# Expert results scattered by choice and token, the last two blocks added by products

## Chip, cores and metric

One core of a Trainium2 chip runs the whole program. The metric is the device time of one execution in microseconds (us).

## What is computed

Two model blocks on 512 tokens of 1024 columns, all in float32. The change touches only the last stage, a mixture of experts: each token picks a group out of 4, and in it the best 2 of 8 experts.

```python
w2 = jax.nn.softmax(top_v, axis=-1) * p_sel            # two shares a token
combine = jnp.sum(one_hot(expert_id, 32) * w2[..., None], axis=1)
for n in range(32):
    a, b = jnp.split(h @ w_up[n], 2, axis=-1)          # 1024 x 512
    out = out + combine[:, n:n + 1] * ((jax.nn.silu(a) * b) @ w_down[n])   # 256 x 1024
x = x + out
```

## The kernel before, in words

Tokens are sorted into *blocks* of up to 96 rows (`ROWS`) that share an expert: 32 first blocks, one for each expert, and up to ten more where an expert has over 96 tokens. With these inputs 32 blocks run: the loads of expert weights stand 32 times in the trace. Token numbers of the slots of all blocks come out of small products of one-hot matrices (`tokens`, L4227): those of the first blocks ahead of block 0, those of the blocks beyond behind block 3.

`experts` (L3999) is one block of five queues. Blocks 0 to 3 are written out (`STATIC`), then a loop on each engine runs pairs of blocks up to a register's value, then the last two, `step((before, 2, 4))` and `step((before, 3, 4))`, are written out again (`each_block`). A block n goes through these steps, spread over neighbouring steps of the loop:

- GpSimd gathers its 96 rows of the normalised tokens from DRAM by an indirect DMA (L4107); in the loop it copies the index column first (L4117). The gather of block n waits until the rows of block n-2 are turned.
- TensorE turns them (`turn_rows`, L4158), multiplies two of eight column groups as float32 (L4169), the other six as three products of a high and a low part (`product`, L399 to L401) with the up weights. ScalarE makes the high parts (L4268, L4276), VectorE the low ones (`rest`, L394).
- ScalarE takes silu, VectorE gates (L4375), TensorE turns the hidden rows (L4183), and `second` multiplies them with the split down weights into banks YB, YB+1.
- ScalarE copies the result to one of two buffers (`result`, L4307); SyncE stores the 96 rows contiguously to `expert_results` in DRAM (L4077), two steps later in its own queue, between the two loads of up weights for block n+2. `result` of n+2 waits for the store of n.

The up weights lie in a ring of two slots of 2 MB, the down weights in two more buffers. Behind the loop `rows_and_shares` (L3968, VectorE) works out in which row of `expert_results` each choice's result lies, and the two shares. Then the block of queues ends, and `combine` (L4428) opens another: GpSimd gathers for each of four token tiles and each of two choices 128 rows by `moe_row` into the ring (eight indirect loads, L4437), VectorE adds each times its share to x (L4448), SyncE stores each tile of x (L4457). The rows of `expert_results` for the ten possible blocks beyond are filled with finite numbers much earlier, by one DMA of 3840 KB in `project_out` (L655).

Of the kernel before, what the change touches and what calls it, by code (L numbers as in the profile page):

```python
# [599 lines left out]
def project_out(k, lhs, tiles, w, gain, next_gain, after=(), scratch=None, x_back=None, router=None):  # L600
# [38 lines left out]
    with ExitStack() as own:  # L639
# [6 lines left out]
        def _(sp):  # L646
# [3186 lines left out]
def number(k, r, pool):  # L3833
# [11 lines left out]
    count(r.sixteens[:, :], [[RUNS, RUN - 1]], RUNS)  # L3845
# [63 lines left out]
def layout(k, r, dve):  # L3909
# [18 lines left out]
    nc.vector.tensor_scalar(r.before_last[:, :], r.more_pairs[:, :], float(NE // 2 - 2), None, ALU.add)  # L3928
# [27 lines left out]
def slots_beyond(k, r, dve):  # L3956
# [8 lines left out]
    nc.vector.tensor_tensor(r.token_of_block[:, :, :], r.is_block[:, :, :], along(r.token_id, shape), ALU.mult).then_inc(r.slotted.sem, 1)  # L3965


def rows_and_shares(k, r, dve):  # L3968
# [4 lines left out]
    shape = [P, 2 * NT, RUN - 1]  # L3973
    nc.vector.tensor_tensor(r.over_one[:, :, :], along(r.rank, shape), across(r.sixteens, shape), ALU.is_gt)
    nc.vector.tensor_scalar(r.row_f[:, :], r.rank[:, :], -1.0, float(RUN), ALU.add, ALU.mult)
    dve.drain()
    nc.vector.tensor_reduce(r.full[:, :].rearrange("p (n o) -> p n o", o=1), r.over_one[:, :, :], AX.X, ALU.add)
    nc.vector.scalar_tensor_tensor(out=r.row_f[:, :], in0=r.block[:, :], scalar=float(ROWS), in1=r.row_f[:, :], op0=ALU.mult, op1=ALU.add)
    dve.drain()
    nc.vector.scalar_tensor_tensor(out=r.row_f[:, :], in0=r.full[:, :], scalar=1.0 - ROWS, in1=r.row_f[:, :], op0=ALU.mult, op1=ALU.add)  # L3980
# [8 lines left out]
    nc.vector.tensor_tensor(r.share2[:, :, :], r.share2[:, :, :], r.share1[:, :, :], ALU.mult)  # L3989

# [8 lines left out]
def experts(k, r, rows_dram, rows_stored, y_dram, up, dn, e):  # L3999
# [7 lines left out]
    XB, UB, YB, HB = 0, 2, 4, 6  # L4007

# [14 lines left out]
    def pair_before_last(queue):  # L4023
        return queue.value_load(r.before_last[0:1, 0:1], min_val=0, max_val=NB // 2 - 2)
# [15 lines left out]
    def later(n, d):  # L4040

        return (n[0], n[1] + d, n[2]) if isinstance(n, tuple) else n + d
# [553 lines left out]
```

## Time and profile before

| | |
|---|---|
| median of 3 runs | 2645.57 us (2643.05 to 2646.64) |
| profiled execution | 2643.07 us |
| its span in the profile | 2641.1 us |
| TensorE busy over the span | 94% |
| VectorE, ScalarE, GpSimd busy | 60%, 43%, 9% |
| expert stage and combine | about 2278 to 2641 us |

The span is what the profiler saw between the first and the last event; the execution's time lies 1.97 us over it. "PE" is TensorE's matrix products, "PEld" its weight loads, DVE is VectorE, ACT ScalarE, POOL GpSimd, SP SyncE. A line of a timeline gives start and duration in us, then engine, line of the kernel, operation and tensors.

### The profile page before, as it was taken

Reading aid. Unit: us, or ns where it says so; the run is one execution under the profiler, and the core shown is the slowest. Engines: PE = TensorE matmul, PEld = TensorE weight load, DVE = VectorE, ACT = ScalarE, POOL = GpSimd, SP = SyncE. Lnnn points to the kernel's source line nnn. Section 1 sums busy time; section 2 is a strip of 40 time slices with the busy share of each in tenths; the row PEclk is TensorE's granted clock in tenths of the full one; section 3 lists DMA queues with packets and bytes.
Section 4 is the critical chain, followed back from the end, with each engine's and each line's share of the span. In section 5 each row is a group of like instructions: output and inputs, shape, how many; then the busy total and the mean of one; then the engine's idle time right before and its main releaser. Section 6 shows DMA issues by size and latency. Waiting matters only on the chain. (4 is left out here: it accounts for less than half of the span.)

```text
span 2641.1 us, 32353 instructions
## 1 busy us (share of the span) xinstructions
PE 2495.4 (94%) x11409; PEld 1903.3 (72%) x11409; DVE 1587.7 (60%) x2386; ACT 1145.1 (43%) x1898; POOL 235.7 (9%) x237
## 2 busy tenths in 40 slices
PE   8999997799999999999999999999899899999995
PEld 6877785577888886766788888678757677666663
DVE  6766445745555525644655553548899656588784
ACT  5423332434444324623444442433333532377773
POOL 0000001000000000000000000345424000111111
PEclk9999999999999999999999999999999999999997
DMA  4321231032333321202233331322202004599995
GB/s 150 108 84 64 96 112 56 31 138 80 96 95 95 128 104 53 86 33 82 93 96 96 97 141 49 111 98 85 95 32 96 1 33 133 184 371 377 387 390 200
DMA packets 196720, 320.65 MB, mean 121 GB/s; under 512 B 16513, under 2 KB 112673, under 8 KB 196609
## 3 DMA queue, kind: packets, MB, share of 16 engines
q1 hardware_dynamic: 191678, 310.71, 34.1%
q0 software_dynamic: 4736, 8.40, 1.0%
q8 instruction: 69, 1.13, 0.2%
q14 instruction: 42, 0.34, 0.0%
q10 hardware_dynamic: 195, 0.06, 0.0%
HBM read 298.43 MB, written 29.10 MB: 124 GB/s over the span
## 5 line engine op out<-in xcount | busy, mean ns | idle before, releaser
L399 PE MATMUL ps<-ffn_parts 128*128 128x512 f32 x1056 | 411.6, 390 | 2.4 <-DVE ffn_parts L394 1.7
L401 PE MATMUL ps<-ffn_parts 128*128 128x512 f32 x1056 | 410.9, 389 | 0.0
L400 PE MATMUL ps<-ffn_parts 128*128 128x512 f32 x1056 | 410.8, 389 | 0.0
L399 PEld LDWEIGHTS ps<-ffn_parts 128*128 128x128 f32 x1056 | 198.2, 188 | 46.5 <-issue 2.6
L394 DVE TENSOR_TENSOR ffn_parts<-ring,ffn_parts 128x1024 fp32r<-128x1024 f32 x132 | 157.7, 1222 | 117.9 <-ACT ffn_parts L2454 107.4
L401 PEld LDWEIGHTS ps<-ffn_parts 128*128 128x128 f32 x1056 | 198.2, 188 | 41.3
L400 PEld LDWEIGHTS ps<-ffn_parts 128*128 128x128 f32 x1056 | 198.2, 188 | 40.9
L394 POOL TENSOR_TENSOR w_lo<-ring,w_hi 128x512 fp32r<-128x512 f32 (+1 forms) x112 | 161.0, 1442 | 720.8 <-ACT w_hi L558 720.4
L2505 DVE SCALAR_TENSOR_TENSOR y_tmp<-ps,pcol,y_tmp 128x511 f32<-128x511 f32 x88 | 61.9, 745 | 214.0 <-ACT y_tmp L2438 214.0
L1012 ACT CAST front_w_hi<-ring 128x512 fp32r<-128x512 f32 x104 | 64.1, 620 | 214.1 <-PE ps L401 214.0
L394 DVE TENSOR_TENSOR front_w_lo<-ring,front_w_hi 128x512 fp32r<-128x512 f32 x104 | 71.5, 688 | 131.5 <-ACT front_w_hi L1012 131.3
L558 ACT CAST w_hi<-ring 128x512 fp32r<-128x512 f32 (+1 forms) x112 | 68.2, 610 | 185.9 <-PE ps L401 178.4
L316 PE MATMUL ps<-brow,ident 128*128 128x512 f32 x248 | 121.4, 630 | 18.9 <-PEq L1938 4.8
L394 DVE TENSOR_TENSOR expert_up_lo<-ring,expert_up_hi 128x1024 fp32r<-128x1024 f32 x96 | 116.8, 1224 | 4.4 <-ACT expert_up_hi L4268 4.2
L3451 DVE SCALAR_TENSOR_TENSOR conv_gate<-conv_u,pcol,conv_gate 128x512 f32<-128x512 f32 x120 | 114.1, 998 | 2.2 <-issue 0.5
L2438 ACT ACTIVATE y_tmp<-ps,pcol 128x512 f32<-128x512 f32 x88 | 63.7, 774 | 109.7 <-PE ps L401 109.5
L4268 ACT CAST expert_up_hi<-ring 128x1024 fp32r<-128x1024 f32 x96 | 101.0, 1054 | 19.7 <-PE ps L401 17.4
L399 PE MATMUL ps<-kept_hi,w_hi 128*128 128x512 f32 x256 | 101.6, 397 | 3.7 <-POOL w_lo L394 2.5
L399 PE MATMUL ps<-front_h_hi,front_w_hi 128*128 128x512 f32 (+1 forms) x232 | 97.4, 420 | 3.8 <-ACT hst L1341 2.7
L399 PE MATMUL ps<-wo_hi,lhs_hi 128*128 128x512 f32 x256 | 100.7, 393 | 0.4 <-DVE lhs_lo L394 0.4
L400 PE MATMUL ps<-kept_lo,w_hi 128*128 128x512 f32 x256 | 100.5, 393 | 0.0
L401 PE MATMUL ps<-kept_hi,w_lo 128*128 128x512 f32 x256 | 100.4, 392 | 0.0
(666 smaller groups left out, 5561.9 us busy)
## 6 DMA issues: line engine op xcount, KB each, us to landing
ring<-in_w_up SPq DMA_DIRECT2D x32, 1536.0 KB, 9.4
ring<-in_ffn_w_up SPq DMA_DIRECT2D x88, 512.0 KB, 5.0
moe_down<-in_w_down SPq DMA_DIRECT2D x32, 1024.0 KB, 10.5
ring<-in_ab_w_in SPq DMA_DIRECT2D x13, 2048.0 KB, 7.9
ring<-in_w_in SPq DMA_DIRECT2D x11, 2048.0 KB, 7.8
ring<-in_ffn_w_down SPq DMA_DIRECT2D x10, 2048.0 KB, 7.7
ring<-in_w_up SPq DMA_DIRECT2D x32, 512.0 KB, 10.2
ring<-in_c_w_in SPq DMA_DIRECT2D x6, 2048.0 KB, 8.1
```

What stands on the lines that cost most here:

```text
L316: k.nc.tensor.matmul(k.ps[:, bank, :], k.ident[:, :], k.brow[:, 0:BANK], start=True, stop=True)
L394: return engine.tensor_tensor(lo, whole, hi.bitcast(F32), ALU.subtract)
L399: nc.tensor.matmul(out, left[0], right[0], start=start, stop=False, **more)
L400: nc.tensor.matmul(out, left[0], right[1], start=False, stop=False, **more)
L401: return nc.tensor.matmul(out, left[1], right[0], start=False, stop=stop, **more)
L558: nc.scalar.copy(part(w_hi, p), chunk(j)[:, rows, cols]).then_inc(k.w_hi_ready.sem, 1)
L1012: k.nc.scalar.copy(self.part(0, p), self.raw(p)).then_inc(k.w_hi_ready.sem, 1)
L2438: last = nc.scalar.activation(ybuf[:, s, half, :], bank(s, half), ACT.Identity, bias=column(bias, i, s, half), scale=column(tap1, i, s, half))
L2505: nc.vector.scalar_tensor_tensor(out=ybuf[:, s, half, 1:T], in0=bank(s, half)[:, 0:T - 1], scalar=column(tap0, i, s, half), in1=ybuf[:, s, ...
L3451: nc.vector.scalar_tensor_tensor(out=y[:, j, :], in0=u[:, j, i:i + T], scalar=tap[:, n:n + 1], in1=y[:, j, :], op0=ALU.mult, op1=ALU.add)
L4268: nc.scalar.copy(e.up_hi[:, 2 * q:2 * q + 2, :], up[s][:, 2 * q:2 * q + 2, :]).then_inc(e.up_cast, 1)
```

## The change

The DRAM tensor of results has a row for each choice and token (2 x 512) instead of one for each slot of a block.

- Each slot gets, beside its token's number, the number of its row of results (`results`, eight more small products at each of the two places). Behind its gather of block n+4, GpSimd scatters the result of block n to these rows by an indirect DMA (`hand_out`); empty slots have a number out of bounds and are left out. SyncE's stores are gone.
- The last two blocks are not scattered. GpSimd waits until all scatters up to the block before them have landed and until the ring's slots are read, and releases SyncE (`free_ring`), which loads the results of choice 0 and 1 for each token tile in order, 512 KB each, with direct DMAs, while the last two blocks are computed.
- The shares are computed behind block 3 (`shares_of_blocks`); a choice whose block is one of the last two has share 0 for the loaded rows, and its share, split in two parts, is moved to the slots by eight small products. ScalarE and VectorE scale the last two results by it and split them, and TensorE adds them up by token: 32 products of one-hot rows (96 x 128) with the high and low parts (96 x 512), in banks `MIXED`.
- VectorE adds eight loaded tiles and four tiles of these products to x, in a written order; SyncE stores the tiles. There is no second block of queues. The DRAM tensor is filled beforehand by one DMA of 4096 KB.

The core of the diff (left out are tile allocations, semaphore names and lines that only rename):

```diff
@@ project_out, SyncE @@
-                sp.dma_start(router.y_beyond, gnext[0:ROWS, :].rearrange("p (o d) -> p o d", o=1).to_broadcast([ROWS, MORE, D])).then_inc(k.param_loaded.sem, 16)
+                sp.dma_start(router.y_rows, gnext[:, :].rearrange("p (o d) -> p o d", o=1).to_broadcast([P, 2 * NT, D])).then_inc(k.param_loaded.sem, 16)
@@ number, layout, slots_beyond @@
-    count(r.sixteens[:, :], [[RUNS, RUN - 1]], RUNS)
+    count(r.result_id[:, :], [[T, 2], [P, NT]], -NO_TOKEN, 1)
+    count(r.ids[:, :], [[1, T]], 0)
...
-    nc.vector.tensor_scalar(r.before_last[:, :], r.more_pairs[:, :], float(NE // 2 - 2), None, ALU.add)
+    for n in range(2):
+        nc.vector.tensor_scalar(r.before_last[:, n:n + 1], r.more_pairs[:, :], float(NE // 2 - 2 - 2 * n), None, ALU.add)
...
+    nc.vector.tensor_tensor(r.token_of_block[:, :, :], r.is_block[:, :, :], along(r.token_id, shape), ALU.mult)
+    nc.vector.tensor_tensor(r.result_of_block[:, :, :], r.is_block[:, :, :], along(r.result_id, shape), ALU.mult).then_inc(r.slotted.sem, 1)
@@ rows_and_shares becomes shares_of_blocks @@
-def rows_and_shares(k, r, dve):
+def shares_of_blocks(k, r, dve):
...
     nc.vector.tensor_reduce(r.below[:, :, :], r.ex[:, :, :], AX.X, ALU.add)
     nc.vector.tensor_scalar(r.share1[:, :, :], r.share2[:, :, :], 1.0, None, ALU.add)
+    for b in range(2):
+        nc.vector.tensor_scalar(r.last[:, b:b + 1], r.more_pairs[:, :], 2.0, float(NE - 2 + b), ALU.mult, ALU.add)
     dve.drain()
-    nc.vector.tensor_copy(r.row[:, :], r.row_f[:, :])
     nc.vector.tensor_tensor(r.below[:, :, :], r.below[:, :, :], r.share1[:, :, :], ALU.mult)
     dve.drain()
     nc.vector.reciprocal(r.share1[:, :, :], r.below[:, :, :])
     dve.drain()
     nc.vector.tensor_tensor(r.share2[:, :, :], r.share2[:, :, :], r.share1[:, :, :], ALU.mult)
+    dve.drain()
+    shares = r.shares[:, :, 0]
+    for out, block, relation in ((r.share_of_last[:, :, 0], 0, ALU.is_equal), (r.share_of_last[:, :, 1], 1, ALU.is_equal), (r.share_before[:, :], 0, ALU.is_lt)):
+        nc.vector.scalar_tensor_tensor(out=out, in0=r.block[:, :], scalar=r.last[:, block:block + 1], in1=shares, op0=relation, op1=ALU.mult)
+    dve.drain()
+    nc.vector.tensor_copy(r.share_parts[:, :, 0:2], r.share_of_last[:, :, :])
+    dve.drain()
+    nc.vector.tensor_tensor(r.share_parts[:, :, 2:4], r.share_of_last[:, :, :], r.share_parts[:, :, 0:2], ALU.subtract).then_inc(r.shares_split.sem, 1)
@@ experts @@
+    MIXED = (2, 6, 4, 0)
...
+    def at_slot(b):
+        return (e.x_hi, e.x_lo)[b][0:ROWS, 0, :, :].rearrange("p c m -> p (c m)")[:, 0:T]
+
+    def last_but_one(n):
+        return isinstance(n, tuple) and n[1:] == (2, 4)
@@ SyncE @@
-                if inside(n, -2):
-                    store(later(n, -2))
...
-            store((before, 2, 4))
-            store((before, 3, 4))
-
-            sp.wait_ge(e.y_ended, 32)
+            for t in range(NT):
+                if t % 2 == 0:
+                    sp.wait_ge(*r.ring_free(t // 2 + 1))
+                for s in range(2):
+                    at = s * T + t * P
+                    sp.dma_start(picked[:, 2 * t + s, :], y_dram[at:at + P, :]).then_inc(r.row_picked[2 * t + s], 16)
+            for t in range(NT):
+                sp.wait_ge(*r.combined(t + 1))
+                sp.dma_start(tiles[:, t, :], k.x[:, t, :]).then_inc(k.param_loaded.sem, 16)
+            sp.wait_ge(*k.param_loaded(16 * NT))
@@ GpSimd @@
+            def scatter(n, index):
+                nc.gpsimd.indirect_dma_start(y_dram, bass.IndirectOffsetOnAxis(ap=index, axis=0), e.y[0:ROWS, side(n), :], None, bounds_check=2 * T - 1, oob_is_err=False)\
+                    .then_inc(e.y_stored[side(n)], 16)
+
+            def hand_out(n):
+                s = side(n)
+                pool.wait_ge(e.y_ready, at_block(n, 1, 1))
+                if not isinstance(n, tuple):
+                    scatter(n, r.result[0:ROWS, n:n + 1])
+                    return
+                nc.gpsimd.tensor_copy(e.slot_result[0:ROWS, s:s + 1], r.result[0:ROWS, bass.ds(at_block(n), 1)])
+                pool.drain()
+                scatter(n, e.slot_result[0:ROWS, s:s + 1])
+
+            def free_ring():
+                for s in range(2):
+                    pool.wait_ge(e.y_stored[s], pairs_before((before, 6, 8)))
+                for n in ((before, 6, 8), (before, 7, 8)):
+                    pool.wait_ge(e.up_split, at_block(n, SPLITS, SPLITS))
+                    pool.wait_ge(e.whole_done, at_block(n, 1, 1))
+                    nc.gpsimd.sem_inc(r.ring_free.sem, 1)
...
+            nc.gpsimd.tensor_tensor(r.result_of[:, :, :], r.one[:, of_choice(1), :], along(r.result_id[:, of_choice(1)], [P, NT, NE]), ALU.mult).then_inc(r.marked.sem, 1)
...
-            before = pair_before_last(nc.gpsimd)
-            each_block(pool, before, lambda n: step(n) if isinstance(n, tuple) or n >= 4 else None, lambda n: after(n) if n > 3 else None, STATIC_ROWS)
+            for n in range(4, STATIC_ROWS):
+                step(n)
+                hand_out(n - 4)
+                after(n)
+            before = nc.gpsimd.value_load(r.before_last[0:1, 1:2], min_val=NE // 2 - 4, max_val=NB // 2 - 4)
+            with pool.Fori(STATIC_ROWS // 2 - 2, NB // 2 - 3) as i:
+                with pool.If(i <= before):
+                    for b in range(2):
+                        step((i, 4 + b, 0))
+                        hand_out((i, b, 0))
+            for b in range(2):
+                step((before, 6 + b, 8))
+                hand_out((before, 2 + b, 8))
+            for b in range(2):
+                hand_out((before, 4 + b, 8))
+            free_ring()
@@ TensorE @@
+                bank = YB
+                if isinstance(n, tuple) and n[1:] == (3, 4):
+                    bank = XB
+                    pe.wait_ge(*r.shares_read(1))
+                elif not early(n, 1):
...
+                if last_but_one(n):
+                    shares_of_slots()
...
+            def results(out, early, late):
+                for t in range(2 * NT):
+                    last = nc.tensor.matmul(out, r.is_slot[:, t, :], early[:, t, :] if t < NT else late[:, t - NT, :], start=(t == 0), stop=(t == 2 * NT - 1), skip_group_check=True)
+                last.then_inc(r.results_found.sem, 1)
...
+                    results(k.ps[0:ROWS, NBANKS - 1, MORE:2 * MORE], r.result_of_block, r.result_of_block[:, NT:2 * NT, :])
+
+            def shares_of_slots():
+                pe.wait_ge(*r.shares_split(1))
+                for t in range(2 * NT):
+                    last = nc.tensor.matmul(k.ps[0:ROWS, XB, 0:4], r.is_slot[:, t, :], r.share_parts[:, t, :], start=(t == 0), stop=(t == 2 * NT - 1))
+                last.then_inc(r.shares_moved.sem, 1)
+
+            def mixed(t, b, half):
+                out, at = k.ps[:, MIXED[t] + half, :], slice(half * BANK, (half + 1) * BANK)
+                for n, y in enumerate((e.dn_hi, e.dn_lo)):
+                    last = nc.tensor.matmul(out, at_slot(b)[:, t * P:(t + 1) * P], y[0:ROWS, 0, b, at], start=(b == 0 and n == 0), stop=(b == 1 and n == 1),
+                                            skip_group_check=True)
+                if b == 1 and half == 1:
+                    last.then_inc(r.mixed.sem, 1)
...
+            pe.wait_ge(*r.results_split(2))
+            for t in range(NT - 1):
+                for half in range(2):
+                    mixed(t, 0, half)
+            for half in range(2):
+                pe.wait_ge(*r.results_split(3 + half))
+                mixed(0, 1, half)
+            for t in range(1, NT):
+                for b in ((1,) if t < NT - 1 else (0, 1)):
+                    for half in range(2):
+                        mixed(t, b, half)
@@ ScalarE @@
+            def last_result(b, n):
+                act.wait_ge(*r.shares_read(1))
+                act.wait_ge(e.down_done, at_block(n, 1, 1))
+                for half in range(2):
+                    at = slice(half * BANK, (half + 1) * BANK)
+                    nc.scalar.activation(e.dn_hi[0:ROWS, 0, b, at], k.ps[0:ROWS, (YB, XB)[b] + half, :], ACT.Copy, scale=r.share_of_slot[0:ROWS, b:b + 1]).then_inc(r.results_cast.sem, 1)
...
+                    split_hidden(later(n, 1))
+                    last_result(0, n)
+                    last_result(1, later(n, 1))
@@ VectorE @@
+                    slots_of_last(n)
                 if inside(n, 1):
                     gated(later(n, 1))
+                    shares_of_slots()
+                    split_hidden(later(n, 1))
+                    split_result(0)
+                    return
...
+            def slots_of_last(n):
+                dve.wait_ge(*r.tokens_read(2))
+                dve.wait_ge(e.up_done, at_block(n, SPLITS, SPLITS))
+                nc.vector.tensor_copy(r.last_token[0:ROWS, :], r.token[0:ROWS, bass.ds(at_block(n), 2)])
+                dve.drain()
+                for b in range(2):
+                    nc.vector.tensor_scalar(at_slot(b), r.ids[0:ROWS, :], r.last_token[0:ROWS, b:b + 1], None, ALU.is_equal)
+
+            def shares_of_slots():
+                dve.wait_ge(*r.shares_moved(1))
+                nc.vector.tensor_reduce(r.share_of_slot[0:ROWS, :].rearrange("p (b o) -> p b o", o=1), k.ps[0:ROWS, XB, 0:4].rearrange("p (h b) -> p b h", b=2),
+                                        AX.X, ALU.add).then_inc(r.shares_read.sem, 1)
+                dve.drain()
+
+            def split_result(b):
+                for half in range(2):
+                    at = slice(half * BANK, (half + 1) * BANK)
+                    dve.wait_ge(*r.results_cast(2 * b + half + 1))
+                    nc.vector.scalar_tensor_tensor(out=e.dn_lo[0:ROWS, 0, b, at], in0=k.ps[0:ROWS, (YB, XB)[b] + half, :], scalar=r.share_of_slot[0:ROWS, b:b + 1],
+                                                   in1=e.dn_hi[0:ROWS, 0, b, at], op0=ALU.mult, op1=ALU.subtract).then_inc(r.results_split.sem, 1)
+
+            def add_picked(t, choices):
+                for s in choices:
+                    dve.wait_ge(r.row_picked[2 * t + s], 16)
+                    nc.vector.scalar_tensor_tensor(out=k.x[:, t, :], in0=picked[:, 2 * t + s, :], scalar=r.share_before[:, s * NT + t:s * NT + t + 1], in1=k.x[:, t, :],
+                                                   op0=ALU.mult, op1=ALU.add)
+                    dve.drain()
+
+            def add_mixed(t):
+                dve.wait_ge(*r.mixed(t + 1))
+                nc.vector.tensor_tensor(k.x[:, t, :], k.x[:, t, :], k.ps[:, MIXED[t]:MIXED[t] + 2, :].rearrange("p a b -> p (a b)"), ALU.add).then_inc(r.combined.sem, 1)
-            rows_and_shares(k, r, dve)
-
-
-def combine(k, r, y_dram, picked, out):
...
+            add_picked(0, (0, 1))
+            add_picked(1, (0,))
+            split_result(1)
+            add_picked(1, (1,))
+            add_picked(2, (0, 1))
+            add_mixed(0)
+            add_picked(3, (0, 1))
+            for t in range(1, NT):
+                add_mixed(t)
```

## Rows read from the trace of the kernel before

**Rows 1.** page, the line over its first part
```profile
span 2641.1 us, 32353 instructions
```

**Rows 2.** busy time by stretch: steady blocks, loop exit; PEclk is the granted clock, then DMA share, GB/s
```profile
2350.00:2594.00 244.00, 244.00 (x1136) 161.71 (x1135) 196.16 (x259) 187.39 (x282) 27.85 (x48) 1.00 1.00 378
2594.90:2601.00 6.10, 4.11 (x7) 1.81 (x8) 2.46 (x4) 3.13 (x5) 0.00 (x0) 0.72 0.22 64
```

**Rows 3.** timeline, one steady block: start us, us, engine, line; idle before in brackets
```profile
2563.64 0.18 POOL L4117 COPY expert_slot_token<-moe_token 96x1 int32 x1 [7.43 <-PE ps L4158]
...
2564.73 0.98 POOL L4107 DMA_INDIRECT y_tmp<-normalised_rows,expert_slot_token  x1 [0.92 <-issue]
...
2566.29 1.07 ACT L4307 COPY y_tmp<-ps 96x512 f32<-96x512 f32 x2 [1.07 <-PE ps L401]
...
2568.55 2.36 DVE L394 TENSOR_TENSOR expert_down_lo<-moe_down,expert_down_hi 128x1024 fp32r<-128x1024 f32 x2 [0.59 <-ACT expert_down_hi L4299]
...
2573.13 0.18 POOL L4117 COPY expert_slot_token<-moe_token 96x1 int32 x1 [7.41 <-PE ps L4158]
```

**Rows 4.** chain that ended last: start us, us, what
```profile
2628.15 8.54 DMA ring<-expert_results,moe_row
...
2636.72 1.28 DVE x_tm L4448
```

**Rows 5.** timeline, from the loop's exit to the combine
```profile
2596.89 3.10 PE L4169 MATMUL ps<-ring,expert_x_whole 128*96 128x512 f32 x4 [2.01 <-issue]
...
2607.29 0.33 PE L4183 MATMUL ps<-ident,h_cm 96*128 96x96 f32 x2
...
2608.52 0.33 ACT L4291 CAST expert_hid_hi<-ps 128x192 fp32r<-128x192 f32 x1
...
2609.34 0.45 PE L399 MATMUL ps<-expert_down_hi,expert_hid_hi 128*96 128x512 f32 x1 [1.72 <-DVE expert_hid_lo L394]
...
2611.93 0.39 PE L401 MATMUL ps<-expert_down_hi,expert_hid_lo 128*96 128x512 f32 x1
2612.36 1.06 ACT L4307 COPY y_tmp<-ps 96x512 f32<-96x512 f32 x2 [3.51 <-PE ps L401]
2617.78 0.97 POOL L4437 DMA_INDIRECT ring<-expert_results,moe_row  x1 [42.57 <-PEq L4432]
...
2624.65 1.80 POOL L4437 DMA_INDIRECT ring<-expert_results,moe_row  x1 [0.30 <-issue]
```

**Rows 6.** groups of instructions, last stage: count | busy us, mean ns | idle before
```profile
L4448 DVE SCALAR_TENSOR_TENSOR x_tm<-ring,moe_share,x_tm 128x1024 f32<-128x1024 f32 x8 | 10.3, 1285 | 16.8 <-DMA ring<-expert_results,moe_row 16.4
...
L787 DVE TENSOR_TENSOR x_tm<-x_tm,ps 128x1024 f32<-128x1024 f32 x4 | 4.9, 1218 | 11.4 <-PE ps L401 11.4
```

**Rows 7.** issue to landing: the stores of results (L4077), and one direct transfer of 2048 KB
```profile
DMA to landing us min/median/max: 3.0/9.5/12.7
...
x_tm<-layer_rows SPq DMA_DIRECT2D x1, 2048.0 KB, 8.2
```

**Rows 8.** timeline, blocks 1 to 4: VectorE's insertion, then TensorE's turns of rows
```profile
2329.40 0.19 DVE L3939 TENSOR_TENSOR moe_over_one<-moe_rank,moe_limits 128x40 f32<-128x40 f32 x1
...
2331.64 2.36 DVE L394 TENSOR_TENSOR expert_down_lo<-moe_down,expert_down_hi 128x1024 fp32r<-128x1024 f32 x2
...
2333.67 0.82 PE L4158 MATMUL ps<-ident,y_tmp 96*128 96x96 f32 x8
...
2343.61 0.83 PE L4158 MATMUL ps<-ident,y_tmp 96*128 96x96 f32 x8
...
2353.79 0.82 PE L4158 MATMUL ps<-ident,y_tmp 96*128 96x96 f32 x8
```

**Rows 9.** timeline, ahead of the first block
```profile
2278.68 0.45 POOL L3836 IOTA moe_slot<- 128x96 f32 x1
...
2282.98 0.40 POOL L4139 TENSOR_TENSOR moe_token_of<-moe_one,moe_token_id 128x128 fp32r<-128x128 f32 x1 [2.84 <-DVE moe_one L3863]
...
2295.82 0.88 PE L4158 MATMUL ps<-ident,y_tmp 96*128 96x96 f32 x8 [2.58 <-DMA y_tmp<-normalised_rows,moe_token]
```

More of the change, by code:

```diff
@@ L4007, in experts @@
     XB, UB, YB, HB = 0, 2, 4, 6
+    MIXED = (2, 6, 4, 0)
+    tiles = out.rearrange("o (t p) d -> p (o t) d", p=P)
     def side(n):
@@ L4193, in second @@
                     for j in range(FTE):
-                        last = product(nc, k.ps[0:ROWS, YB + half, :], [h[:, s, j * ROWS:(j + 1) * ROWS] for h in (e.hid_hi, e.hid_lo)],
+                        last = product(nc, k.ps[0:ROWS, bank + half, :], [h[:, s, j * ROWS:(j + 1) * ROWS] for h in (e.hid_hi, e.hid_lo)],
                                        [w[:, s, j, half * BANK:(half + 1) * BANK] for w in (e.dn_hi, e.dn_lo)], j == 0, j == FTE - 1)
@@ L4414, in _ @@
             columns(0)
+            dve.wait_ge(*r.results_found(1))
+            nc.vector.tensor_scalar(r.result[0:ROWS, 0:NE], k.ps[0:ROWS, 5, 0:NE], float(NO_TOKEN), None, ALU.add).then_inc(r.results_read.sem, 1)
             split_down(0)
@@ L4516, in moe @@
         r.more = sb("moe_more", [P, MORE, 1], to=c)
-        r.desc, r.own, r.slot, r.limits, r.beyond, r.evens, r.count, r.blocks, r.end, r.start, r.pairs, r.more_pairs, r.bar, r.sixteens = (
+        r.desc, r.own, r.slot, r.limits, r.beyond, r.evens, r.count, r.blocks, r.end, r.start, r.pairs, r.more_pairs, r.bar = (
             sb("moe_" + name, [P, w], to=c) for name, w in (("falling", NE), ("own", NE), ("slot", ROWS), ("limits", MOST - 1), ("beyond", MORE), ("evens", MORE // 2),
                                                             ("count", NE), ("blocks", NE), ("block_end", NE), ("block_start", NE), ("pairs", MORE // 2),
-                                                            ("more_pairs", 1), ("bar", 1), ("sixteens", RUN - 1)))
-        r.token_id, r.rank, r.full, r.block, r.ahead, r.row_f = (
-            sb("moe_" + name, [P, 2 * NT], to=c) for name in ("token_id", "rank", "full", "block", "ahead", "row_f"))
-        r.row = sb("moe_row", [P, 2 * NT], I32, to=c)
+                                                            ("more_pairs", 1), ("bar", 1)))
+        r.token_id, r.result_id, r.rank, r.full, r.block, r.ahead, r.share_before = (
+            sb("moe_" + name, [P, 2 * NT], to=c) for name in ("token_id", "result_id", "rank", "full", "block", "ahead", "share_before"))
         r.expert = sb("moe_expert", [P, NB], I32, to=c)
-        r.before_last = sb("moe_before_last", [P, 1], I32, to=c)
-        r.token = sb("moe_token", [P, NB], I32, to=c)
+        r.before_last = sb("moe_before_last", [P, 2], I32, to=c)
+        r.token, r.result = (sb("moe_" + name, [P, NB], I32, to=c) for name in ("token", "result"))
         r.falling, r.numbered, r.group_found, r.below_top, r.chosen, r.marked = k.ga, k.da, k.mean_ready, k.root_ready, k.vb, k.norm_ready
```

86 lines of the change are left out of this document (32 added, 54 removed).

## The prediction

> **What bounds the kernel now.** I read the page first: one core, a span of 2641.1 us [rows 1]. The change touches the last stage, the 32 blocks of 96 expert rows and the combine behind them, so two readings are needed: the steady blocks, and everything behind the last of them.
>
> In the steady blocks TensorE is the bound [rows 2]: 244.00 us busy in 244.00 us, at the full clock. VectorE is busy 196.16 of them and ScalarE 187.39. The DMA engines are busy all the time as well, at 378 GB/s, but nothing waits for them there. A block takes 9.49 us: that is the distance between two of GpSimd's index copies [rows 3]. So a part that only takes bytes or SyncE issues out of the blocks buys nothing. A part that makes VectorE late costs only what goes past its idle time, (244.00 - 196.16) over 25.7 blocks = 1.9 us in each.
>
> Behind the last block the chain is serial [rows 4, 5]: TensorE's last product ends near 2612.3, ScalarE copies it out until 2613.42 (2612.36 + 1.06), SyncE stores it, it lands in 3.0 us [rows 7], the block closes, and GpSimd starts the first of eight indirect loads at 2617.78. They are issued one by one, some 1.0 to 1.8 us each. The last lands 8.54 us after its start and VectorE's last addition ends at 2638.00. The span ends 3.10 us later with the store of the output. From the last product to the end are 28.8 us, with TensorE idle. The profiled execution took 2643.07 us, 1.97 over its span.
>
> **What the change does to this tail.** I set the same clock times again, step by step.
>
> *Start of the loads.* The result of block 29 is copied out at 2567.36 + 3 x 9.49 = 2595.83 (ScalarE's two copies end at 2567.36 for block 26 [rows 3]; block 29 is three later). GpSimd then copies the index (0.18), drains and issues: the gather began 1.09 after its index copy began and took 0.98 [rows 3], so the scatter is issued by 2598. A store behind the loop landed in 3.0 us [rows 7], so about 2601. `free_ring` then also wants the four unsplit products of block 31, 2596.89 to 2599.99 [rows 5]; that is earlier. So SyncE issues the eight loads of 512 KB from 2601.2. A direct transfer of 2048 KB took 8.2 us [rows 7]; two in a row give 16.4 as a bound, and if their fixed part overlaps 12 to 14. All rows are there between 2613 and 2617.6, the first at about 2605. VectorE wants its last pair only at 2621, so the loads stay hidden. The 4 MB with which the result buffer is filled beforehand (3.84 before) lie 400 us ahead of its use.
>
> *The last two products.* Ahead of `second` of block 30, TensorE does eight matmuls for the shares, at 0.085 apart (8 tables cost 0.69, below): +0.7. The product then ends, and the turn of block 31's hidden rows starts at 2607.29 + 0.7 = 2608.0 [rows 5]. ScalarE now casts it at once (before, it came behind the 1.07 us copy of result 30, at 2608.52), so at 2608.35; +0.33, VectorE's half 0.36 behind. Second product at 2609.2, against 2609.34 before: no change. It ends at 2612.1. VectorE's one-hot rows (two compares of 96x512) lie where it waits for block 31's first product, ahead of the gating; they cost nothing, some 1.3 us if that cover were gone.
>
> *Split of result 30.* ScalarE casts two halves from 2608.7 (0.54 each, by the two copies of the same shape in [rows 3]), VectorE subtracts each (half a 1218 ns addition from PSUM [rows 6], so 0.61, 0.7 with its wait): ready at 2610.7. Here VectorE starts to add.
>
> *VectorE's list.* Eight additions of loaded rows: 1.285 [rows 6], with the drain 1.34: 10.7. Split of result 31: 1.3 (ScalarE's casts end at 2613.4, before it is reached). Four additions from PSUM at 1.22: 4.9. Sum 16.9, with a few waits 17.0. So VectorE ends at 2627.7.
>
> *TensorE's 32 split products* have VectorE's list to hide under. At full rate (the last product's twelve begin in 2609.34 to 2611.93, eleven steps of 0.235 [rows 5]) they take 7.5 us, from 2612.1 and with a wait for result 31 until about 2620; tile 0 is wanted at 2620, tiles 1 to 3 behind 2624. Hidden.
>
> *End.* 2627.7 + 3.10 = 2630.8. **The tail gives 10.3 us.**
>
> **What the change adds ahead of it.**
> - Behind block 3 eight more matmuls on TensorE, for the result rows. The eight for the tokens stand there now: turns of rows 2343.61 to 2353.79 are 10.18 apart where a block takes 9.49 [rows 8], so eight cost 0.69. I take 0.7.
> - `shares_of_blocks` moves from the end (where it lay beside the last product, free) to VectorE behind block 3: seven dependent steps and some more, estimated at 2.3 us. A like insertion, `blocks_of_choices`, took 2329.40 to 2331.64 = 2.24 us, and the turns stand 9.94 apart there: 0.45 lost [rows 8]. Here TensorE is held up itself by 1.4 us of small matmuls, so VectorE has more room: between 0 and 0.45, I take 0.2.
> - Ahead of the first block: GpSimd counts 512 ids. The 96-wide count took 0.45 [rows 9], by width at most 2.4; then it would hold GpSimd until 2282.1, and its multiplication begins at 2282.98 behind 2.84 us of waiting for VectorE. Nothing. Its third multiplication (0.40) lies in the wait for the tokens. TensorE's eight more matmuls (0.7) lie ahead of a wait of 2.58 us for the first gathered rows [rows 9]: nothing; 0.7 without that cover.
> - In each block GpSimd gets a second copy and issue, 0.18 + 0.9 + 0.98 = 2.1 us from 2567.36; the next gather is not due until 2573.13 [rows 3], and it is wanted a block and a half after that. Result n+2 is written into the same buffer 2 x 9.49 - 1.07 = 17.9 us after result n is ready; issue 2.1 and the 9.5 us that a store takes to land under load (the median, [rows 7]) are less. Nothing. SyncE loses 32 stores and their wait, which stood ahead of the load of the unsplit weights. No one waits for these loads, so nothing is gained.
>
> Where the scatter falls there is one thing to weigh. The combine's issue at 2624.65 took 1.80 [rows 5], beside a VectorE addition with both inputs in SBUF, where the others took 0.95. The scatter will start near 2568.5, just where VectorE splits the down weights for 2.36 us, both inputs in SBUF [rows 3]. With 1.80 GpSimd is done at 2570.4, still before 2573.13: by one price as by the other the sum has nothing. The Trainium skill, page "SBUF — State Buffer", section "Who interferes with whom", speaks against the change here: such a VectorE instruction and a GpSimd instruction that reads SBUF shut each other out for a whole instruction, whichever starts first. By that rule GpSimd's 1.80 is no accident, and the trace agrees, but VectorE can be held as well; this is the third rival.
>
> **Sum:** 10.3 - 0.7 - 0.2 = 9.4 us. 2643.07 - 9.4 = 2633.7 for an execution like the profiled one; the median of the three runs stands 2.5 higher, so I say **2636.2**.
>
> **The rivals.**
> 1. *The loads become the bound.* Scatter 29 and the loads must be 5 us later than above before VectorE waits at the end. If the scatter lands in the 12.7 us of the slowest store instead of 3.0 [rows 7] and the loads run like the indirect ones (18.9 us from first issue to last landing [rows 4, 5]), they end at 2610.9 + 18.9 = 2629.8; plus 1.34 + 3 x 1.22 + 3.10 is 2637.9. Saved 3.2 - 0.9 = 2.3: 2643.3. Against it: the queues are empty by then and the loads are contiguous. With one of the two late it is as forecast.
> 2. *A slow tail.* Leaving the loop cost TensorE 2.01 us of "issue" [rows 5] and the clock fell to a mean of 0.72 [rows 2]. The new code behind the loop is longer and TensorE waits in it. At 1.2 GHz 32 products take 15.0 us instead of 7.5: they end at 2627.6 with the wait, VectorE at 2628.8, +1.1; a second stop of 2 us on VectorE's list makes it +3.1. Saved 6.3: 2639.3.
> 3. *Slower: the scatters hold VectorE in the blocks.* 2.24 us put on VectorE cost TensorE 0.45. If each scatter (copy, issue, both locking) costs VectorE that much, 28 blocks with a full block behind them lose 28 x 0.45 = 12.6 us: net +3.2, 2648.8. It decides from 0.34 us a block (9.4/28), so from some 2.1 us of VectorE time; one issue of 0.98 can hold it for no more than that. Unlikely.
> 4. *The front costs more, or the tail less is won, each by 2 to 3 us*: within 5.3 us of no change.
>
> **How the numbers follow.** 0.2% is 5.3 us, about what a measurement of this kernel can tell from no change. Forecast 0.67, rival 1 0.08, rival 2 0.13, rival 3 0.06, rival 4 0.06. Faster than 2640.3: forecast and rival 2, and a little over from the others, 0.82; within: 0.12; slower: rival 3, 0.06. Low end: no cost in front (0.9), no stop at the loop's exit (2.0), runs at the lowest of the three (2.5 below the median): about 2631.5. High end: between rivals 2 and 1, 2642.5.
>
> **What would show it.** Right: no combine stage; VectorE's list unbroken from 2610.7 less the shift to its end 17 us later; all eight direct loads landed before it waits; SyncE's last store 3.1 us before the end; turns of rows 9.49 apart, one gap of about 11.1 behind block 3. Wrong: waits of VectorE for DMA between its additions (rival 1), TensorE's products above 0.4 us apart and VectorE waiting for TensorE at tiles 1 to 3 (rival 2), blocks longer than 9.49 with VectorE ahead of TensorE's waits (rival 3).

## The result, and the profile after

The changed kernel took 2687.98 us (median of 4 runs, 2686.41 to 2691.19) where the kernel before took 2645.82 on the same chip: ratio 1.0163, 95% interval 1.0150 to 1.0176. I had forecast 2636.2 in a range of 2631.5 to 2642.5. It is 42 us slower where I had forecast some 9 us less.

The windows of the changed kernel over the looped blocks (columns: window, length, then PE, PEld, DVE, ACT and POOL busy with their counts, granted clock, DMA share, GB/s):

```profile
2370.00:2640.00 270.00, 238.30 (x1012) 152.73 (x1011) 174.17 (x230) 166.58 (x253) 53.74 (x89) 0.94 0.82 292
```

TensorE was busy all the time before, at the full clock [rows 2]. Now it is idle 31.7 us of 270, and the clock falls to a mean of 0.94 with it. No engine is full. GpSimd, with 53.74 us busy, looks the least suspicious of all. The waits of the stage say otherwise (us in total, times, longest):

```profile
POOL results_of_choices L4130 <- issue: 165.2, 26, 8.2
...
POOL y_tmp L4115 <- issue: 68.5, 25, 6.2
...
PE ps L4203 <- DMA y_tmp<-normalised_rows,expert_slot_token: 31.7, 20, 3.0
```

TensorE waits in nearly every looped block for rows that GpSimd gathered too late. GpSimd in turn stands for 234 us in "issue": idle time that no semaphore ended. Part 4 of the profile's page has the same word on top of the chain that ended last:

```profile
issue 8%; PE 3%; POOLq 2%; DVE 1%; DMA 0%; POOL 0%; DVEq 0%; ACT 0%; ACTq 0%
```

GpSimd's timeline shows where in the block it stands (start, duration, engine, line; in brackets the idle time ahead and what ended it), to be held against [rows 3]:

```profile
2553.15 0.94 POOL L4130 DMA_INDIRECT results_of_choices<-y_tmp,expert_slot_result  x1 [6.83 <-issue]
2554.09 0.20 POOL L4125 COPY expert_slot_token<-moe_token 96x1 int32 x1
2557.04 0.99 POOL L4115 DMA_INDIRECT y_tmp<-normalised_rows,expert_slot_token  x1 [2.74 <-issue]
2558.02 0.20 POOL L4139 COPY expert_slot_result<-moe_result 96x1 int32 x1
2564.91 0.95 POOL L4130 DMA_INDIRECT results_of_choices<-y_tmp,expert_slot_result  x1 [6.69 <-issue]
```

Between each index copy and the issue behind it stands one `pool.drain()` (L4126, L4140). Ahead of the scatter it takes 6.69 us, ahead of the gather 2.74. With the two copies and two issues a round is 0.20 + 2.74 + 0.99 + 0.20 + 6.69 + 0.95 = 11.77 us; a block was 9.49. GpSimd has become the bound while it does nothing. What it waits for can be read from TensorE's turn of the rows gathered at 2557.04:

```profile
2564.07 1.28 PE L4203 MATMUL ps<-ident,y_tmp 96*128 96x96 f32 x8 [2.02 <-DMA y_tmp<-normalised_rows,expert_slot_token]
```

These rows are there at about 2564.07. The chain that ended last gives the first instruction of GpSimd's queue (POOLq) behind the drain, and it starts 0.06 us after that:

```profile
2564.13 0.03 POOLq L4130
```

The scatter's own row follows at 2564.91. The static blocks ahead of the loop have no copy and no drain. There the scatter follows a gather in flight with no such stop:

```profile
2320.60 0.99 POOL L4115 DMA_INDIRECT y_tmp<-normalised_rows,moe_token  x1 [2.92 <-PE ps L4203]
2324.52 0.96 POOL L4130 DMA_INDIRECT results_of_choices<-y_tmp,moe_result  x1 [2.93 <-ACT y_tmp L4392]
```

The trace has the drains themselves too, as records of the queue that do not count as busy (count: shortest/median/longest in ns, first and last start). Ahead of the gather and ahead of the scatter in the changed kernel, then ahead of the gather in the kernel before:

```profile
L4126 POOLq DRAIN  x24: 1223/3040/7099, 2359.8 to 2639.7; - x24
L4140 POOLq DRAIN  x26: 2338/7098/8584, 2363.7 to 2653.0; - x26
L4118 POOLq DRAIN  x24: 320/326/587, 2354.8 to 2573.1; - x24
```

A record is longer than the idle time in the brackets because it begins while the issue ahead of it is still running. The same instruction took 0.33 us before and takes 3.0 or 7.1 now.

The theory from this, called D below: a drain on GpSimd lasts until the indirect transfers that GpSimd has already issued have landed. The tail, on the other hand, is the one that was forecast (VectorE's list; it answers to [rows 4, 5]):

```profile
2665.27 1.40 DVE L4537 SCALAR_TENSOR_TENSOR expert_down_lo<-ps,moe_share_of_slot,expert_down_hi 96x512 fp32r<-96x512 f32 x2 [0.23 <-ACT expert_down_hi L4400]
2666.59 3.99 DVE L4543 SCALAR_TENSOR_TENSOR x_tm<-ring,moe_share_before,x_tm 128x1024 f32<-128x1024 f32 x3
...
2679.90 3.48 DVE L4549 TENSOR_TENSOR x_tm<-x_tm,ps 128x1024 f32<-128x1024 f32 x3
```

**Where the time went**, in the profiled executions. The spans are cut at TensorE's turns of hidden rows. From that of block 4 to that of block 29, where the loop ends: 237.3 us before (2357.24 to 2594.56), 289.4 after (2362.24 to 2651.61), +52.0. From the exit to the end: 46.5 before, 35.2 after, -11.35. The insertion behind block 3: +0.7. That is 41.4 together; the spans differ by 45.7. The rest lies ahead of the stage, where the change alters only the size of one DMA: GpSimd's first count of the stage began at 2282.91 in this execution and at 2278.47 before. In the kernels below it began between 2277.16 (e5, with the larger DMA) and 2283.60 (e3, with the smaller one), so these 4.4 are variation between executions.

Of the 11.35 about 1.05 is not the tail that was planned. From the exit to the turn of the last hidden rows this execution took 12.4 us, at a granted clock of 1.00; e2, e4 and e8 took 13.4 there, at 0.87, and the kernel before 12.7, at 0.87. From the exit to the end e8 took 36.3 us, 10.2 less than before.

### The profile page after: what moved, and what is told of

It reads as the page before. It is cut to its first block and busy times, and to the rows that moved or that the text cites. A ratio compares the mean times of both kernels' runs of the same rounds, so it can differ in the third digit from the quotient of the medians.

```text
span 2686.8 us, 32527 instructions
## 1 busy us (share of the span) xinstructions
PE 2528.9 (94%) x11465; PEld 1922.8 (72%) x11465; DVE 1596.2 (59%) x2402; ACT 1144.5 (43%) x1899; POOL 267.5 (10%) x287
```

## The experiments

Each kernel is timed against the kernel before on its own chip: e1 to e4 on one (before: 2645.24), e5 to e8 on a second (2645.92), e9 on a third (2645.50). So kernels of different groups are compared by their ratios as well. Their edits are against the changed kernel unless said otherwise. The code shown leaves out that in all of them but e3 and e4 each looped issue is preceded by raising a semaphore that nobody waits for. e1 and e2 both have it, so it is not what tells them apart.

**One drain in place of two, and none between gather and scatter** (`e1_one_drain`; the two scatters behind the loop keep their copy and drain):

```diff
+ if isinstance(n, tuple):          # step: ahead of the wait for the turned rows
+     tensor_copy(slot_token ...); tensor_copy(slot_result ...)
+     pool.drain()
  pool.wait_ge(e.turned, at_block(n, 1, -1))
- tensor_copy(slot_token ...); pool.drain()      # step
- tensor_copy(slot_result ...); pool.drain()     # hand_out, in the loop
```

**The same with one bare drain put back** between gather and scatter (`e2_drain_back`: `+ pool.drain()` in `hand_out`).

> The changed kernel, with both index copies and one drain ahead of GpSimd's wait for the turned rows, so that no drain stands between a gather and the scatter behind it. Theory D (a drain on GpSimd waits until the indirect DMAs issued before it have landed): the gap between gather and scatter in the loop falls from some 6.5 us to the wait for the result, blocks are 9.5 us apart again, and the time is what the tail gives, 2634 to 2640 us. Rival I (GpSimd gets its instructions late in a longer dynamic loop): as many instructions are left, so blocks stay near 11.7 us and the time near 2688. Rival Q (an indirect DMA itself waits for the one before it in its queue): the scatter still starts some 6 us behind the gather, near 2685.

> The same as the kernel with one drain, but one more drain between the gather and the scatter, with no copy to wait for. Theory D: the scatter starts 0.9 us behind the gather's landing again, blocks 11 to 12 us, time 2675 to 2695. Rivals I and Q: no change against the kernel with one drain.

Measured: e1 2636.38 us (2632.63 to 2642.06), ratio 0.9965 [0.9953, 0.9976]; e2 2690.31, ratio 1.0168 [1.0147, 1.0188]. GpSimd's timeline of e2, then of e1:

```profile
2450.89 0.99 POOL L4115 DMA_INDIRECT y_tmp<-normalised_rows,expert_slot_token  x1 [2.81 <-issue]
2458.95 0.95 POOL L4131 DMA_INDIRECT results_of_choices<-y_tmp,expert_slot_result  x1 [7.08 <-issue]
```
```profile
2446.57 0.98 POOL L4115 DMA_INDIRECT y_tmp<-normalised_rows,expert_slot_token  x1 [5.18 <-issue]
2448.13 0.94 POOL L4131 DMA_INDIRECT results_of_choices<-y_tmp,expert_slot_result  x1 [0.58 <-issue]
```

In e1 gather and scatter go out 1.56 us apart, both in flight at once, and the block is 9.49 again (scatters at 2448.13 and 2457.62). One bare drain, with no copy ahead of it, brings back the 7 us gap and the whole 54 us. Both kernels lie where theory D had them. So it is the drain, not the second indirect transfer, not the index copy, not bandwidth.

The one drain that e1 keeps is not cheap. It stands behind the scatter, with gather and scatter in flight, and its record has a median of 7.3 us:

```profile
L4123 POOLq DRAIN  x24: 5558/7302/9727, 2353.0 to 2576.1; - x24
```
```profile
POOL y_tmp L4115 <- issue: 114.4, 21, 7.2
```

The second line is from the list of waits between 2370 and 2590: some 5 us idle in each block. It does no harm, because 7.3 us fit into a block of 9.49 us, and the 3.0 and 7.1 us of the changed kernel together do not: TensorE is busy 220.00 of 220.00 us in that window.

**A drain's price, measured in the kernel before** (`e3_probe`). It adds work that is of no use: a copy, a drain and a copy behind each looped gather, into a spare tile.

```diff
  gather(n, e.slot_token[...])
+ nc.gpsimd.tensor_copy(e.probe[0:ROWS, 0:1], r.slot[0:ROWS, 0:1])
+ pool.drain()
+ nc.gpsimd.tensor_copy(e.probe[0:ROWS, 1:2], r.slot[0:ROWS, 0:1])
```

> The kernel before, with a small copy, a drain and a second small copy behind each looped gather, and nothing else. Theory D: the two copies stand as far apart as the gather is in flight, 5 to 7 us, in all 24 looped blocks; the time stays within 2643 to 2649, since GpSimd has 8 us of idle time a block there. Rivals I and Q: the copies stand less than 0.5 us apart.

Measured: 2645.68 us, ratio 0.9999 [0.9989, 1.0009]. Its timeline, then the wait over the stage and the drain's own record:

```profile
2408.20 0.98 POOL L4107 DMA_INDIRECT y_tmp<-normalised_rows,expert_slot_token  x1 [0.84 <-issue]
2409.18 0.93 POOL L4120 COPY probe<-moe_slot 96x1 f32<-96x1 f32 x1
2414.72 0.89 POOL L4122 COPY probe<-moe_slot 96x1 f32<-96x1 f32 x1 [4.62 <-issue]
```
```profile
POOL probe L4122 <- issue: 118.9, 24, 6.4
```
```profile
L4121 POOLq DRAIN  x24: 6126/6741/8448, 2360.9 to 2579.8; - x24
```

From the start of the gather's issue to the end of the drain are 2414.72 - 2408.20 = 6.5 us, where a gather took 6.4 (median, in the kernel before) to land. Five of these lie idle in every block and the kernel is no slower, since GpSimd had 7.4 us to spare in it. That is why nothing of this shows in the kernel before: there the loop's drain comes 8.6 us behind the start of the last gather's issue and finds nothing in flight. It takes 0.33 us of the 0.92 that [rows 3] shows ahead of the gather.

**The order turned round** (`e4_swap`: `hand_out` ahead of `step` in the loop).

> The changed kernel with two lines swapped in GpSimd's loop and in its last pairs: the scatter of block n ahead of the gather of block n+4; same instructions, both drains left. Theory D: the drain ahead of the scatter now meets a gather that is issued a block earlier and has landed, the one ahead of the gather meets the scatter (2.7 us); about 6 us of GpSimd a block, so blocks of 9.5 us and 2634 to 2641 us. Rival I: the same instructions take as long, near 2688. Rival Q: gather behind scatter waits 2 us, scatter behind gather nothing, so fast as well; it is told from D by the drain put back.

Measured: 2692.5 us, ratio 1.0174 [1.0158, 1.0191]. A miss of mine. I had reasoned as if a round began anew in each block. The round is a cycle: scatter, drain, gather, drain, and either order has both drains in it, one behind each transfer; their records have medians of 3.1 us ahead of the gather and 6.4 ahead of the scatter.

```profile
2549.30 0.99 POOL L4115 DMA_INDIRECT y_tmp<-normalised_rows,expert_slot_token  x1 [2.50 <-issue]
...
2557.83 0.94 POOL L4130 DMA_INDIRECT results_of_choices<-y_tmp,expert_slot_result  x1 [7.34 <-issue]
```

**Semaphores in place of the drains** (`e8_semaphores`). The index copy raises a semaphore itself and GpSimd waits for that alone; likewise for the result's index:

```diff
- nc.gpsimd.tensor_copy(slot_token ...)
- pool.drain()
+ nc.gpsimd.tensor_copy(slot_token ...).then_inc(e.token_copied.sem, 1)
+ pool.wait_ge(e.token_copied.sem, at_block(n, 1, 1))
```

> The changed kernel with the two drains in GpSimd's loop replaced by a wait on a semaphore that the copy itself raises: same copies, same order, nothing else waits. Theory D: gather, copy, scatter follow each other within 1 us where their own waits allow, no gap of 6.5 us, blocks of 9.5 us, time 2634 to 2640 us. Rivals I and Q: still above 11 us a block and above 2680 us.

Measured: 2635.24 us (2633.97 to 2640.26), ratio 0.9965 [0.9951, 0.9979].

```profile
2443.75 0.18 POOL L4125 COPY expert_slot_token<-moe_token 96x1 int32 x1 [3.59 <-PE ps L4209]
2444.79 0.99 POOL L4115 DMA_INDIRECT y_tmp<-normalised_rows,expert_slot_token  x1 [0.86 <-POOL expert_slot_token L4125]
2447.63 0.18 POOL L4140 COPY expert_slot_result<-moe_result 96x1 int32 x1 [1.85 <-ACT y_tmp L4398]
2448.70 0.95 POOL L4131 DMA_INDIRECT results_of_choices<-y_tmp,expert_slot_result  x1 [0.89 <-POOL expert_slot_result L4140]
```
```profile
2370.00:2590.00 220.00, 220.00 (x1022) 145.25 (x1020) 175.69 (x231) 169.60 (x257) 52.83 (x91) 1.00 0.98 359
```

Every stop has a name now: TensorE 3.59, ScalarE 1.85, and 0.86 and 0.89 for its own copies. GpSimd is again idle for want of work, TensorE busy 220.00 of 220.00. All of the change's plan is kept, only the drains are gone, and 52.7 us come back. The Trainium skill, page "GPSIMD Engine Reference", section 2.1 "Instruction dispatch", asks for a wait on the producer's completion semaphore between two Pool instructions where the second reads what another core of GpSimd wrote; e8 is that wait. No run here reads an index without waiting for it; what the trace shows is the wait's price, 0.86 and 0.89 us.

Now the tail. **VectorE's list shortened at its head** (`e5_early_adds`, on e1: `add_picked(0, (0, 1))` moved ahead of `split_hidden` of the last block), **no split products** (`e6_all_scattered`, on e1: all 32 results scattered, the loads behind the last), and **the loads held back** (`e7_loads_held`, on e1: SyncE also waits for the split of result 30):

> The kernel with one drain, and VectorE adds the two loaded tiles of token tile 0 ahead of the low part of block 31's hidden rows, in a wait of 3.08 us. If the first two loads have landed by then (they were issued at 2603.3 and VectorE would want them at 2608.8) the list behind it is 2.7 us shorter: 2633 to 2634.5. If they land later than 2609.2, the hidden rows, the second product and all behind it move back by as much, and little is gained or lost.

> The kernel with one drain, without the split products: the last two blocks are scattered as well, the eight direct loads wait for all scatters, VectorE adds eight tiles. It leaves apart what the scatters and direct loads alone are worth. If my working of the tail holds: result 31 copied out some 1 us later than the last product, scatter issued 2 us behind that, landed 2.5 us later, eight loads in 12.2 us, one addition, 3.5 us of store: 3.5 to 5 us slower than the kernel with one drain, 2640 to 2642, still faster than before. If the split products were what costs, it is faster than 2636.

> The kernel with one drain, its eight loads held back until VectorE begins to add, some 9.2 us later. The prediction had them hidden with a few us to spare at the end: then VectorE waits some 3.5 us for the first and, as a load comes each 1.5 us and an addition takes 1.34, little more: 2 to 4 us slower, 2638.5 to 2640.5. If the loads were not a matter at all, no change; if they were the bound, 9 us slower.

| kernel | median us (range) | ratio to before on its chip | span |
|---|---|---|---|
| e1_one_drain | 2636.38 (2632.63 to 2642.06) | 0.9965 [0.9953, 0.9976] | 2634.0 |
| e5_early_adds | 2632.75 (2629.99 to 2638.2) | 0.9960 [0.9948, 0.9973] | 2628.2 |
| e6_all_scattered | 2641.84 (2639.51 to 2644.73) | 0.9987 [0.9977, 0.9997] | 2642.2 |
| e7_loads_held | 2641.52 (2639.86 to 2643.19) | 0.9984 [0.9974, 0.9993] | 2639.9 |

SyncE's loads and VectorE's list, in e1:

```profile
2603.25 4.94 SPq L4106 DMA_DIRECT2D ring<-results_of_choices  x8
```
```profile
2612.45 1.41 DVE L4541 SCALAR_TENSOR_TENSOR expert_down_lo<-ps,moe_share_of_slot,expert_down_hi 96x512 fp32r<-96x512 f32 x2 [0.23 <-ACT expert_down_hi L4404]
2613.77 3.99 DVE L4547 SCALAR_TENSOR_TENSOR x_tm<-ring,moe_share_before,x_tm 128x1024 f32<-128x1024 f32 x3
```

The loads start 10.5 us ahead of VectorE's first addition (2603.25, 2613.77) and no addition waits for them. In e7 they start 11.4 us later, and VectorE waits 3.47 + 1.33 + 0.42 = 5.2 us for them; its median is 5.1 above e1's, 5.0 by the ratios. I had expected 2 to 4. In e6 the loads start only at 2622.77 and VectorE stands before the first and the third:

```profile
2618.04 1.28 DVE L4548 SCALAR_TENSOR_TENSOR x_tm<-ring,moe_share_before,x_tm 128x1024 f32<-128x1024 f32 x1 [3.47 <-DMA ring<-results_of_choices]
2620.65 1.29 DVE L4548 SCALAR_TENSOR_TENSOR x_tm<-ring,moe_share_before,x_tm 128x1024 f32<-128x1024 f32 x1 [1.33 <-DMA ring<-results_of_choices]
```
```profile
2626.47 2.64 DVE L4518 SCALAR_TENSOR_TENSOR x_tm<-ring,moe_share_before,x_tm 128x1024 f32<-128x1024 f32 x2 [11.65 <-DMA ring<-results_of_choices]
2630.20 8.17 DVE L4518 SCALAR_TENSOR_TENSOR x_tm<-ring,moe_share_before,x_tm 128x1024 f32<-128x1024 f32 x6 [1.09 <-DMA ring<-results_of_choices]
```

(the first pair is e7, the second e6). So of the some 9 us that e1 gains on the kernel before, some 5.5 are from the split products, which let the loads start before the last two results are there (2641.84 - 2636.38; 5.8 by the ratios), and 3 to 4 from the scatters (e6 against before), and loads that start early enough are a condition of the whole. e6 lies inside the 2640 to 2642 that I had expected. In e5 two additions fill VectorE's wait ahead of the last hidden rows:

```profile
2604.81 2.65 DVE L4548 SCALAR_TENSOR_TENSOR x_tm<-ring,moe_share_before,x_tm 128x1024 f32<-128x1024 f32 x2
...
2612.06 1.40 DVE L4542 SCALAR_TENSOR_TENSOR expert_down_lo<-ps,moe_share_of_slot,expert_down_hi 96x512 fp32r<-96x512 f32 x2 [1.07 <-ACT expert_down_hi L4404]
```

2.64 us leave the list and 1.07 come back as a wait for ScalarE. The spans of e1 and e5 differ by 5.8, but e5's stage began 3.8 earlier by the variation told above: the tail itself gave 2.0, the medians 3.6, the ratios 1.3. The intervals overlap, so the times alone do not show the sign; the median is a little below the 2633 to 2634.5 that I had expected.

**Both together** (`e9_sem_early`: e8 with e5's edit).

> The changed kernel with semaphores in place of GpSimd's two drains of the loop, and the two loaded tiles of token tile 0 added ahead of the last block's hidden split. By theory D (the drains were the whole loss of the loop, and VectorE's list behind the last turn is the tail) the two savings are independent: e8_semaphores' 2635.2 less the 2.8 (2.0 to 3.6) that the early adds gave e5_early_adds, so 2632.4, 2631 to 2634; GpSimd's waits in the loop stay on TensorE and ScalarE, and a block stays 9.49. By the rival, that a copy and its semaphore cost something near the end of the loop that one common drain does not, it stays above e5_early_adds by over 2, at 2635 or more.

Measured: 2632.80 us (2630.9 to 2635.61), ratio 0.9956, 95% interval 0.9942 to 0.9969. It is the level of e5 and 2.4 below e8, by the medians as by the ratios, though the two intervals overlap. Counted from GpSimd's first count to the end of the span, e8 takes 353.2 us and e9 351.1, e1 353.0 and e5 351.0: the early additions are worth 2.0 to 2.1 in both pairs. Semaphores and one common drain are worth the same, and the version beats both kernels, the one before by some 12 us and the changed one by 55.

## Why the prediction was wrong

**The step that failed** is this one: "In each block GpSimd gets a second copy and issue, 0.18 + 0.9 + 0.98 = 2.1 us from 2567.36 ... Nothing." The cost put on the drain was wrong. The 0.9 was read from [rows 3] as the fixed price of a drain. It is a wait whose length is what is still in flight: 2.7 us idle behind a scatter, 6.7 behind a gather. And the gather's own drain got longer too, as it now has a scatter 3 us ahead of it. 2.1 us became 0.20 + 6.69 + 0.95, and 0.92 became 2.74, so that GpSimd's round came to 11.77 us in the block shown, where it has 9.49. Over the 22 blocks from TensorE's turn of hidden rows at 2381.22 to that at 2642.11 a block takes 11.86 us, and 22 x (11.86 - 9.49) = 52.1 us is the whole loss of the loop. I priced the drain as an instruction and did not ask what it waits for. In the same sentence lay the overlap that I had wrong: "the next gather is not due until 2573.13" holds only if the scatter's drain is done by then.

The trace of before could have warned me, in a place that I did not read. Behind the loop stands one more drain (L4148), directly behind the last gather. Its rows are the gather's, the drain's (ns), and the gather's time to landing (us):

```profile
2574.23 0.98 POOL L4107 DMA_INDIRECT y_tmp<-normalised_rows,expert_slot_token  x1 [0.92 <-issue]
```
```profile
L4148 POOLq DRAIN  x1: 6560/6560/6560, 2574.0 to 2574.0; - x1
```
```profile
y_tmp<-normalised_rows,expert_slot_token POOLq DMA_INDIRECT x1, 6.3
```

It lasts 6.56 us from 2574.0, to about 2580.6, and that gather lands 6.3 us after its issue at 2574.23, at about 2580.5. The loop's drains take 0.33 in the same trace. The scatter's drain was put at 2567.5, 2.8 us behind the start of a gather's issue [rows 3], so it had to meet a gather in flight, as this one does and the short ones do not. No range of mine held it, and it should have, with landing times of 6.4 to 12.7 us ([rows 7] for the last) as its upper bound.

**Right, by its steps.** The tail: 10.3 us forecast; from the turn of the last hidden rows to the end are 33.8 us before (2607.29 to 2641.1) and 22.8 after (2663.97 to 2686.8), 11.0 less, of which the 0.7 for the shares is to be taken off: 10.3. VectorE's list is unbroken from 2665.27 to 2683.38; from its first addition at 2666.59 it takes 16.8 us (forecast 17.0), and the end is 3.4 us later (forecast 3.10). The matmuls for the result rows: turns of rows in after at 2337.96, 2347.92 and 2358.80, so 10.88 where 10.18 stood: 0.7. VectorE's 0.2 behind block 3 was not seen. The forecast for the whole without the drains is e8: 2635.24 against 2636.2, inside the range. Counted from GpSimd's first count to the end, e8 takes 353.2 us and the kernel before 362.6, so 9.4 less, as forecast: 0.9 more up to the turn of block 4, 0.15 less in the loop, 10.2 less behind it. One sum of mine was off: the three terms of the low end give 2636.2 - 0.9 - 2.0 - 2.5 = 2630.8, not 2631.5.

**The rivals.** 1 (loads the bound) and 2 (slow tail) did not come: no addition of after waited for a load, and TensorE waited 0.58 us in the mixed products, at full clock. Rival 3 had the place, the blocks, and the sign, but not the mechanism nor the size: I had 0.45 us a block through the port. In e8 the scatter does lie beside VectorE's split, and this takes 2.42 us in three blocks in a row (2439.18, 2448.66, 2458.15) instead of [rows 3]'s 2.36: 0.06 us a block on VectorE, and the block stays 9.49. GpSimd pays more of it: 2 of e8's 26 scatters with a copied index took 2.00 us to issue where the median is 0.95. The Trainium skill's section "Who interferes with whom" of the page "SBUF — State Buffer" has one instruction shut the other out whole, but it also says that a tensor_tensor on VectorE was not seen to stall a DMA's issue. The median issue beside the split agrees with the second; the two of 2.00 us and the copies in the last section look like the first. Rival 4 (a dearer front) did not come either: 0.9 in e8, as forecast. I had given a slower end 6 in 100, all of it to a wrong mechanism.

**Open.** Whether a drain waits for the data or for the last completion of its descriptors was not told apart; the drain ends 0.06 us after TensorE takes up the rows, which does not tell them apart. Why the gaps ahead of the looped scatters of after swing between 6.4 and 8.2 us was not tried.

## What to carry to other kernels

A drain has no price of its own, only a condition: ask what can be in flight when it is reached, and price it at that transfer's landing. I would ask the same of any other stop with no operand, though none was run here. Then ask how many such waits stand in one round of the loop: e1 waits as long as the changed kernel does behind its gather, but once in a block, and loses nothing. An idle time called "issue" in a profile is where such a condition hides, and it can be short only because nothing is in flight yet; the drain's own records in the queue, one line for each drain, show whether one of them is long. Between an index copy and the transfer that reads it a semaphore raised by the copy is enough: it cost at most 0.9 us in each of e8's 48 such waits, with a gather in flight or not.

## What the hardware showed that I had not expected

- A drain on GpSimd behind an indirect transfer lasts until about its landing: from the start of the gather's issue to the end of the drain are 6.5 us in e3, where a gather takes 6.5 (median; 6.4 in the kernel before) to land. The drain's own record has a median of 6.7 us there, 7.1 ahead of the scatter in after, 7.3 in e1, and 0.33 in the kernel before with nothing in flight. The transfer's own row shows 0.98. The Trainium skill, page "Perfetto Trace Analysis", section "DMA Instruction — SWDGE (GPSIMD)", says that such a row ends with the writing of descriptors, not with the movement; the trace agrees.
- A 96x1 copy on GpSimd takes longer beside VectorE's split of weights, which has both inputs in SBUF. Between 2350 and 2640 it took 0.18 to 0.23 us wherever no such split ran beside it (128 copies of after, e1, e2, e3 and e8), also directly behind an issue (0.20 at 2554.09 above); beside one it took up to 1.19 in e1 and 1.24 in e3. In the same stretches issues of indirect transfers took at most 0.99 without such a split and up to 2.00 beside one. No experiment took the split away from a copy, so this is read from rows that lie beside each other and not shown by an edit. From e1, a split and the two copies beside it:

```profile
2448.43 2.40 DVE L394 TENSOR_TENSOR expert_down_lo<-moe_down,expert_down_hi 128x1024 fp32r<-128x1024 f32 x2 [0.59 <-ACT expert_down_hi L4388]
2449.06 0.68 POOL L4121 COPY expert_slot_token<-moe_token 96x1 int32 x1
2449.69 1.18 POOL L4122 COPY expert_slot_result<-moe_result 96x1 int32 x1
```
- Two indirect transfers of GpSimd can be in flight at once: in e1 they go out 1.5 to 2.1 us apart, and TensorE never waits for the rows in the loop. It is not free for the second one: a scatter lands in 7.0 us (median) in e1, behind a gather, and in 3.0 in e2, where a drain has let the gather land first.
